# One wait per pair of rows for the diagonals' places on ScalarE, and a Gelu semaphore that counts rows

## The chip, the cores and the metric

The kernel runs on one core of a Trainium2 chip. The metric is the device time of one execution in microseconds (us). Before the change it is 900.75 us, the median of three runs (900.59 to 900.79 us).

## The reference

One decoder block over 256 positions of width 1024, all in float32. Its first half mixes tokens: a modulated RMS norm, one wide input projection, eight heads of forgetting attention and eight heads of causal ALiBi attention, sigmoid gates, an output projection and a gated residual. The change touches only the second half, PEER:

```
h2 = rms_norm(x, norm2_g) * (1 + scale2) + shift2
# per token and head: 16 of 16384 experts by two top-16 searches over 128 keys each
a = einsum('cd,chkd->chk', hc, u_tab[ec])      # dot with each chosen expert's u row
w = gc * gelu(a)                               # gc: softmax of the 16 scores of the head
y = einsum('chk,chkd->cd', w, v_tab[ec])       # weighted sum of the v rows
x = x + gate2 * y
```

With 8 heads and 16 experts a head each token reads 128 rows of u and 128 rows of v, 1024 floats each. The tables lie side by side in HBM, so that one row of 2048 floats holds u and v of an expert.

## The kernel before, in words

The tokens are two tiles of 128, one token to a partition. The engines are programmed one by one, each in its own written order, and meet at semaphores. After the attention and the projections comes the gather stage. It has 256 rows (`ROWS`): row n is expert number n % 128 of each token of tile n // 128, and it is 128 x 2048 floats, 1 MB.

- GpSimd (L594) gathers row n with an indirect DMA into one of 16 places of SBUF. A place is free again once TensorE has added the row that lay there (`s_added`), and the row's expert numbers must be there (`s_eid`).
- VectorE (`dots`, L1016) multiplies the landed u half with `h2` and sums it: `s_dot`.
- ScalarE (`weights_of`) makes from the dot the weight of the expert and a diagonal matrix of it: Gelu of the dots of two rows in one instruction (L1294, `s_gelu`), a product with the softmax value for each row (L1299, `s_ew`), and for each row a copy of the identity scaled by the weight into one of `ND` = 8 places of `diag` (L1306, `s_diag`). A place of `diag` is free once TensorE has added the row of eight rows before.
- TensorE (`add_rows`, L1620) multiplies the diagonal with the v half, two halves of 512 columns, and sums all 128 rows of a tile in PSUM. The profile shows four matmuls for a row, two for each half. It then tells `s_added`.
- After the last row of a tile VectorE (`finish`, L1027 and L1029) adds the gated sum to the residual and SP stores it.

ScalarE takes the rows in pairs (`expert_weights`), apart from the last 8 rows (`ALONE` = 4 pairs), which it takes one by one. Between the pairs of the stage other work is laid at fixed slots (`SLOT`): key queries and their scores on TensorE and ScalarE, the top-16 searches on VectorE up to slot 76, softmax parts on ScalarE. The expert numbers of later heads come out of that work while the rows of earlier heads are gathered.

In `weights_of` two waits stand ahead of each diagonal from row 8 on. ScalarE's instruction can carry one of them itself, and the other is an instruction of its own, which the profile shows as EVENT_SEMAPHORE at L1305. The first four pairs (rows 0 to 7) have no wait for a place.

Of the kernel before, what the change touches and what calls it, by code (L numbers as in the profile page):

```python
# [11 lines left out]
ACT = mybir.ActivationFunctionType  # L12
# [7 lines left out]
TOPK = 16  # L20
# [7 lines left out]
ND = 8  # L28
# [144 lines left out]
def block_kernel(nc, x, small, b_ada, b_fgate, norm2_g, ada_t, in_t, up_t, out_t, peer_t, keys_t, peer_uv, out):  # L173
# [21 lines left out]
    with ExitStack() as ctx:  # L195
        def sb(name, shape, dt=F32):
            return ctx.enter_context(nc.sbuf_tensor(name, shape, dt))

        def sem(name):
            return ctx.enter_context(nc.semaphore(name))  # L200
# [19 lines left out]
        diag = sb("diag", [P, ND, P])  # L220
# [54 lines left out]
        ident = sb("ident", [P, P])  # L275
# [16 lines left out]
        g_sb = sb("g_sb", [P, NG * TOPK])  # L292
# [3 lines left out]
        adot = mask[:, 0:2 * TOPK]  # L296
        gel = mask[:, 2 * TOPK:3 * TOPK]
        ew = mask[:, 3 * TOPK:4 * TOPK]
# [113 lines left out]
        s_dot = sem("dot_ready")  # L412
        s_added = sem("v_row_added")
        s_gelu = sem("gelu_ready")
        s_ew = sem("expert_weights_ready")
# [645 lines left out]
        def _(act):  # L1061
# [221 lines left out]
                gt = g_sb[:, t * P + h * TOPK:t * P + (h + nh) * TOPK]  # L1283
                act.activation(gt, gt, ACT.Exp).then_inc(s_g1, 1)

            gelus = [0]

            def weights_of(rows_):

                first, count = rows_[0], len(rows_)  # L1290
                at = first % (2 * TOPK)
                some = slice(first % TOPK, first % TOPK + count)
                act.wait_ge(s_dot, first + count)
                act.activation(gel[:, some], adot[:, at:at + count], ACT.Gelu_apprx_tanh).then_inc(s_gelu, 1)  # L1294
                gelus[0] += 1
                act.wait_ge(s_gelu, gelus[0])
                for n in rows_:
                    c_ = n % TOPK
                    act.activation(ew[:, c_:c_ + 1], g_sb[:, n:n + 1], ACT.Copy,  # L1299
                                   scale=gel[:, c_:c_ + 1]).then_inc(s_ew, 1)  # L1300
                for n in rows_:
                    c_ = n % TOPK
                    act.wait_ge(s_ew, n + 1)
                    if n >= ND:
                        act.wait_ge(s_added, n - ND + 1)  # L1305
                    act.activation(diag[:, n % ND, :], ident[:], ACT.Copy,  # L1306
                                   scale=ew[:, c_:c_ + 1]).then_inc(s_diag, 1)

            def expert_weights(pair):

                if pair >= NG * PAIRS - ALONE:
                    for n in (2 * pair, 2 * pair + 1):
                        weights_of((n,))
                else:
                    weights_of((2 * pair, 2 * pair + 1))

            behind = {}
            for t in range(TILES):
# [33 lines left out]
            for pair in range(NG * PAIRS):  # L1352
                expert_weights(pair)
                run(pair)
# [351 lines left out]
```

## Time and profile before

| what | us |
|---|---|
| median of three runs | 900.75 |
| profiled execution | 900.84 |
| its span | 899.0 |
| TensorE matmul busy | 779.8 |
| VectorE busy | 613.0 |
| ScalarE busy | 346.6 |
| GpSimd busy | 291.1 |

The span is the time from the first to the last instruction of the program. Matmuls overlap and their ends are modelled, so that TensorE's busy time is not its work at full speed. Waits, branches and DMA issues do not count as busy. The transfers are spread over 16 DMA engines; a DMA share of 1.00 says that all of them had packets under way all the time.

### The profile page before, as it was taken

To read this page: it belongs to the slowest core of one execution; us is meant where nothing else is said; L and a number is where in the kernel's file an instruction comes from. 1 tells how busy PE (TensorE), PEld (TensorE's weight loads), DVE (VectorE), ACT (ScalarE), POOL (GpSimd) and SP (SyncE) were. 2 spreads that over 40 slices of the span, in tenths; PEclk is the share of its full clock that TensorE was granted. 3 is DMA by queue.
4 is the path that set the end of the run, shared out by engine and by line. 5 is a ranking of instruction groups with operands and counts; after the bars stand their busy time and mean duration, and the time that the engine had idled before them with its cause. 6 is when DMAs were issued, how large, how long until landed. Compare 5 with 4: busy or idle time off the path is not lost.

```text
span 899.0 us, 8440 instructions
## 1 busy us (share of the span) xinstructions
PE 779.8 (87%) x2526; PEld 420.1 (47%) x2526; DVE 613.0 (68%) x1420; ACT 346.6 (39%) x1027; POOL 291.1 (32%) x279
## 2 busy tenths in 40 slices
PE   4999999999999999999997888787777777777777
PEld 2377877667556556565652333333323232223232
DVE  6788798964587967748669788668744444444445
ACT  3458687862244342423423232322322222222222
POOL 4000000000244454553546344453443434333320
PEclk9999999999999999999998888898899999999999
DMA  9978454689499999999999999999999999999995
GB/s 371 425 268 296 160 208 195 236 337 397 150 387 422 390 423 420 411 421 421 421 421 421 421 422 420 422 422 420 422 421 422 421 423 420 421 423 422 421 422 217
DMA packets 44100, 336.70 MB, mean 375 GB/s; under 512 B 4884, under 2 KB 5012, under 8 KB 7320
## 3 DMA queue, kind: packets, MB, share of 16 engines
q0 software_dynamic: 37152, 268.45, 72.1%
q1 hardware_dynamic: 6888, 67.72, 19.1%
q8 instruction: 20, 0.33, 0.1%
q14 instruction: 24, 0.20, 0.1%
q10 hardware_dynamic: 16, 0.00, 0.0%
HBM read 335.11 MB, written 1.05 MB: 374 GB/s over the span
## 4 chain that ended last, share of the span: by engine, by line
PE 49%; DMA 35%; DVE 10%; ACT 3%; issue 2%; POOL 1%; SPq 0%; DVEq 0%; POOLq 0%; ACTq 0%
DMA ring<-in_peer_uv,eid 26%; PE ps_y L1620 22%; DMA rows<-in_peer_uv,eid 6%; PE bank L1590 6%; PE bank L1556 3%; DVE ring L1016 3%; PE bank L1431 2%; PE bank L1433 2%; PE bank L1432 2%; DMA ring<-in_ada_t 2%; PE bank L1571 2%; PE ps_y L1431 1%; PE ps_y L1433 1%; PE ps_y L1432 1%; PE bank L1476 1%
## 5 line engine op out<-in xcount | busy, mean ns | idle before, releaser
L1620 PE MATMUL ps_y<-ring,diag 128*128 128x512 f32 x572 | 282.0, 634 | 57.2 <-ACT diag L1306 57.2
L594 POOL DMA_INDIRECT ring<-in_peer_uv,eid x142 | 159.0, 1119 | 421.5 <-DVE eid L922 225.0
L1016 DVE CUSTOM_DVE_ANT_0 ring<-ring,gates 128x1024 f32<-128x1024 f32 x143 | 173.3, 1225 | 102.3 <-DMA ring<-in_peer_uv,eid 101.5
L1620 PEld LDWEIGHTS ps_y<-ring,diag 128*128 128x128 f32 x572 | 111.5, 201 | 208.7 <-issue 122.2
L1294 ACT ACTIVATE mask<-mask 128x2 f32<-128x2 f32 (+1 forms) x132 | 26.7, 203 | 374.3 <-DVE mask L1016 374.1
L1306 ACT ACTIVATE diag<-ident,mask 128x128 f32<-128x128 f32 x256 | 87.3, 387 | 0.3
L1620 PE MATMUL ps_y<-rows,diag 128*128 128x512 f32 x136 | 61.8, 597 | 7.6 <-ACT diag L1306 7.6
L1299 ACT ACTIVATE mask<-g_sb,mask 128x1 f32<-128x1 f32 x256 | 61.9, 287 | 4.3
L1016 DVE CUSTOM_DVE_ANT_0 rows<-rows,gates 128x1024 f32<-128x1024 f32 x34 | 41.3, 1224 | 31.7 <-DMA rows<-in_peer_uv,eid 31.6
L651 DVE TENSOR_TENSOR w_lo<-ring,w_hi 128x512 fp32r<-128x512 f32 x76 | 50.8, 686 | 11.0 <-PE bank L1433 9.4
L1111 ACT ACTIVATE w_hi<-ring 128x512 fp32r<-128x512 f32 x76 | 45.6, 626 | 24.5 <-PE bank L1433 23.9
L636 DVE SCALAR_TENSOR_TENSOR rows<-ring,silu,rows 128x512 f32<-128x512 f32 x64 | 47.7, 749 | 3.3 <-DMA ring<-in_ada_t 2.2
L1620 PE MATMUL ps_y<-kz,diag 128*128 128x512 f32 x88 | 40.1, 598 | 5.6 <-ACT diag L1306 5.6
L1620 PEld LDWEIGHTS ps_y<-rows,diag 128*128 128x128 f32 x136 | 25.2, 190 | 41.9 <-issue 27.0
L594 POOL DMA_INDIRECT rows<-in_peer_uv,eid x34 | 35.5, 1043 | 26.7 <-PE ps_y L1620 21.1
L1620 PE MATMUL ps_y<-gates,diag 128*128 128x512 f32 x72 | 34.6, 602 | 7.7 <-ACT diag L1306 7.7
L1016 DVE CUSTOM_DVE_ANT_0 kz<-kz,gates 128x1024 f32<-128x1024 f32 x22 | 26.7, 1224 | 18.8 <-DMA kz<-in_peer_uv,eid 18.8
L1431 PE MATMUL bank<-w_hi,hT_hi 128*128 128x512 f32 x88 | 36.1, 410 | 0.0
L1433 PE MATMUL bank<-w_lo,hT_hi 128*128 128x512 f32 x88 | 34.3, 390 | 0.0
L1432 PE MATMUL bank<-w_hi,hT_lo 128*128 128x512 f32 x88 | 34.3, 390 | 0.0
L594 POOL DMA_INDIRECT kz<-in_peer_uv,eid x22 | 22.7, 1032 | 32.7 <-PE ps_y L1620 19.2
L1620 PE MATMUL ps_y<-spare,diag 128*128 128x512 f32 x52 | 25.2, 606 | 8.9 <-ACT diag L1306 7.6
(229 smaller groups left out, 1191.2 us busy)
## 6 DMA issues: line engine op xcount, KB each, us to landing
ring<-in_ada_t SPq DMA_DIRECT2D x11, 2048.0 KB, 9.8
ring<-in_in_t SPq DMA_DIRECT2D x10, 2048.0 KB, 10.5
ring<-in_up_t SPq DMA_DIRECT2D x2, 2048.0 KB, 7.7
ring<-in_out_t SPq DMA_DIRECT2D x2, 2048.0 KB, 10.8
ring<-in_peer_uv,eid POOLq DMA_INDIRECT x142, 28.6
x_sb<-in_x SPq DMA_DIRECT2D x2, 1024.0 KB, 10.1
ring<-in_ada_t SPq DMA_DIRECT2D x2, 1024.0 KB, 21.4
kz<-in_peer_t SPq DMA_DIRECT2D x1, 2048.0 KB, 19.2
```

The source lines that it names most:

```text
L594: pool.indirect_dma_start(uv_row(n), None, peer_uv, bass.IndirectOffsetOnAxis(ap=eid[:, n:n + 1], axis=0)).then_inc(s_uv[name], 16)
L636: ins = dve.scalar_tensor_tensor(out=acc, in0=w, scalar=silu[:, k:k + 1], in1=acc, op0=ALU.mult, op1=ALU.add)
L651: dve.tensor_tensor(w_lo[:, j % NLO, :], w, w_hi[:, j % NHI, :].bitcast(F32), ALU.subtract).then_inc(s_w_lo, 1)
L1016: dve.tensor_tensor_reduce(u_row(n), u_row(n), h2[:, n // P, :], 1.0, 0.0, ALU.mult, ALU.add, adot[:, at:at + 1]).then_inc(s_dot, 1)
L1111: act.activation(w_hi[:, j % NHI, :], ring[:, no % NW, k, :], ACT.Copy).then_inc(s_w_hi, 1)
L1299: act.activation(ew[:, c_:c_ + 1], g_sb[:, n:n + 1], ACT.Copy, scale=gel[:, c_:c_ + 1]).then_inc(s_ew, 1)
L1306: act.activation(diag[:, n % ND, :], ident[:], ACT.Copy, scale=ew[:, c_:c_ + 1]).then_inc(s_diag, 1)
L1431: pe.matmul(spot, hT_hi[:, k, at], hi, start=(k == 0), stop=False)
L1432: pe.matmul(spot, hT_lo[:, k, at], hi, start=False, stop=False)
L1433: ins = pe.matmul(spot, hT_hi[:, k, at], lo, start=False, stop=(k == KD - 1))
L1590: ins = pe.matmul(b[:, j * P:(j + 1) * P], peer_block(m // 2, k)[:, at:at + P], tT[:, t, k, :], start=(k == 0), stop=(k == KD - 1))
L1620: ins = pe.matmul(ps_y[:, cut], diag[:, n % ND, :], v_row(n)[:, cut], start=first, stop=last)
```

## The change

`weights_of` takes numbers (first row, how many, and the row for the semaphore counts) in place of a list. For a pair, it waits for a place of `diag` once, for the second row of the pair, and that wait stands ahead of the second product (L1299) and no longer ahead of the two diagonals. Since rows are added in order, that count covers the first row's place too. For a single row the wait stands ahead of its product. `s_gelu` goes up by the number of rows of the Gelu, and not by one.

```diff
-            gelus = [0]
-            def weights_of(rows_):
-                first, count = rows_[0], len(rows_)
+            def weights_of(first, count, row):
                 at = first % (2 * TOPK)
                 some = slice(first % TOPK, first % TOPK + count)
-                act.wait_ge(s_dot, first + count)
-                act.activation(gel[:, some], adot[:, at:at + count], ACT.Gelu_apprx_tanh).then_inc(s_gelu, 1)
-                gelus[0] += 1
-                act.wait_ge(s_gelu, gelus[0])
-                for n in rows_:
-                    c_ = n % TOPK
-                    act.activation(ew[:, c_:c_ + 1], g_sb[:, n:n + 1], ACT.Copy,
+                act.wait_ge(s_dot, row + count)
+                act.activation(gel[:, some], adot[:, at:at + count], ACT.Gelu_apprx_tanh).then_inc(s_gelu, count)
+                act.wait_ge(s_gelu, row + count)
+                for r in range(count):
+                    c_ = first % TOPK + r
+                    if r == count - 1 and first >= ND:
+                        act.wait_ge(s_added, row + (count - ND))
+                    act.activation(ew[:, c_:c_ + 1], g_sb[:, row + r:row + r + 1], ACT.Copy,
                                    scale=gel[:, c_:c_ + 1]).then_inc(s_ew, 1)
-                for n in rows_:
-                    c_ = n % TOPK
-                    act.wait_ge(s_ew, n + 1)
-                    if n >= ND:
-                        act.wait_ge(s_added, n - ND + 1)
-                    act.activation(diag[:, n % ND, :], ident[:], ACT.Copy,
+                for r in range(count):
+                    c_ = first % TOPK + r
+                    act.wait_ge(s_ew, row + (r + 1))
+                    act.activation(diag[:, (first + r) % ND, :], ident[:], ACT.Copy,
                                    scale=ew[:, c_:c_ + 1]).then_inc(s_diag, 1)
...
                     for n in (2 * pair, 2 * pair + 1):
-                        weights_of((n,))
+                        weights_of(n, 1, n)
                 else:
-                    weights_of((2 * pair, 2 * pair + 1))
+                    weights_of(2 * pair, 2, 2 * pair)
```

## Rows read from the trace of the kernel before

**Rows 1.** The kernel in three stretches: busy us of each engine, clock, DMA share, GB/s.
```profile
core 0: us, PE busy (x) PEld busy (x) DVE busy (x) ACT busy (x) POOL busy (x), PEclk, DMA share, GB/s
250.00:400.00 150.00, 147.45 (x621) 88.15 (x620) 113.66 (x308) 57.01 (x181) 78.39 (x64) 1.00 1.00 410
400.00:884.00 484.00, 391.97 (x950) 170.15 (x948) 306.20 (x717) 141.10 (x510) 197.55 (x189) 0.94 1.01 421
884.00:899.00 15.00, 9.39 (x20) 3.55 (x20) 7.60 (x12) 3.80 (x13) 0.00 (x0) 1.00 0.30 118
```

**Rows 2.** The last loop of the chain of waits: start us, us, what.
```profile
813.72 33.45 DMA ring<-in_peer_uv,eid
847.19 1.23 DVE ring L1016
849.51 2.00 PE ps_y L1620 x4
851.77 0.94 POOL extra L594
853.49 33.44 DMA ring<-in_peer_uv,eid
886.95 1.23 DVE ring L1016
889.23 4.57 PE ps_y L1620 x10
893.83 0.70 DVE tmp L1027
```

**Rows 3.** GpSimd in order of time, 489 to 499 us: start, us, idle before, releaser.
```profile
490.63 0.96 POOL L594 DMA_INDIRECT ring<-in_peer_uv,eid  x1 [0.60 <-PE ps_y L1620]
498.86 0.93 POOL L594 DMA_INDIRECT ring<-in_peer_uv,eid  x1 [7.27 <-PE ps_y L1620]
```

**Rows 4.** The stretch between these two gathers.
```profile
490.63:498.86 8.23, 4.05 (x5) 1.85 (x6) 6.50 (x14) 2.53 (x10) 0.96 (x1) 0.63 1.01 422
```

**Rows 5.** The waiting instruction of L1305 over the run: duration min/median/max, first and last start.
```profile
L1305 ACTq EVENT_SEMAPHORE  x248: 17/17/17, 280.9 to 890.9; - x124
```

**Rows 6.** ScalarE's first pair in order of time, rows 0 and 1, without L1305.
```profile
252.93 0.20 ACT L1294 ACTIVATE mask<-mask 128x2 f32<-128x2 f32 x1 [4.78 <-DVE mask L1016]
253.17 0.30 ACT L1299 ACTIVATE mask<-g_sb,mask 128x1 f32<-128x1 f32 x1
253.37 0.28 ACT L1299 ACTIVATE mask<-g_sb,mask 128x1 f32<-128x1 f32 x1
253.56 0.39 ACT L1306 ACTIVATE diag<-ident,mask 128x128 f32<-128x128 f32 x1
253.85 0.39 ACT L1306 ACTIVATE diag<-ident,mask 128x128 f32<-128x128 f32 x1
```

**Rows 7.** A later pair of ScalarE in order of time, with L1305 ahead of both diagonals.
```profile
602.98 0.20 ACT L1294 ACTIVATE mask<-mask 128x2 f32<-128x2 f32 x1 [3.67 <-DVE mask L1016]
603.22 0.29 ACT L1299 ACTIVATE mask<-g_sb,mask 128x1 f32<-128x1 f32 x1
603.42 0.28 ACT L1299 ACTIVATE mask<-g_sb,mask 128x1 f32<-128x1 f32 x1
603.61 0.39 ACT L1306 ACTIVATE diag<-ident,mask 128x128 f32<-128x128 f32 x1
603.90 0.39 ACT L1306 ACTIVATE diag<-ident,mask 128x128 f32<-128x128 f32 x1
```

**Rows 8.** ScalarE in order of time, one of the last eight rows.
```profile
885.72 0.20 ACT L1294 ACTIVATE mask<-mask 128x1 f32<-128x1 f32 x1 [1.52 <-DVE mask L1016]
885.96 0.29 ACT L1299 ACTIVATE mask<-g_sb,mask 128x1 f32<-128x1 f32 x1
886.29 0.40 ACT L1306 ACTIVATE diag<-ident,mask 128x128 f32<-128x128 f32 x1
```

**Rows 9.** From the start to 335.60 us: TensorE's matmuls of L1620, then ScalarE's L1299.
```profile
0.00:335.60 335.60, 51.86 (x117) 0.99 0.78 310
0.00:335.60 335.60, 7.89 (x34) 0.99 0.78 310
```

**Rows 10.** Who waited for ScalarE's diagonals, 250 to 400 us: total us, times, longest.
```profile
PEld ps_y L1620 <- ACT diag L1306: 6.0, 11, 2.2
PE ps_y L1620 <- ACT diag L1306: 1.9, 2, 1.4
```

**Rows 11.** VectorE: L983 for one head, then for two, each with its successor.
```profile
277.50 0.17 DVE L983 SCALAR_TENSOR_TENSOR eid<-score 128x16 int32<-128x16 f32 x1
277.59 0.16 DVE L986 TENSOR_REDUCE gsum<-g_sb 128x1 f32<-128x16 f32 x1
314.14 0.19 DVE L983 SCALAR_TENSOR_TENSOR eid<-score 128x32 int32<-128x32 f32 x1
314.25 0.18 DVE L986 TENSOR_REDUCE gsum<-g_sb 128x2 f32<-128x32 f32 x1
```

## The prediction, made before the changed kernel ran

> **What bounds the kernel now.** I read the stretches first, the chain of waits second, and then ScalarE instruction by instruction. From 400 to 884 us the DMA engines have packets all the time (share 1.01) and move 421 GB/s, while TensorE is busy 392 of 484 us, VectorE 306 and ScalarE 141 [rows 1]. A gathered row is 128 x 8192 bytes = 1.049 MB, so it takes 1.049 / 421 = 2.49 us, and 484 / 2.49 = 194 rows pass in that stretch. The transfers bound it. From 250 to 400 us the rate is 410 GB/s: (421 - 410) / 421 x 150 = 3.9 us worth of bytes fewer, and there TensorE is busy 147.5 of 150 us [rows 1]. What lies before 250 us has no instruction of the change. Behind 884 us come the last rows and the store.
>
> The chain of waits looks otherwise at first sight: it runs in loops from a transfer (33.4 us) over VectorE, ScalarE and TensorE to GpSimd, which issues the next transfer into the place that came free [rows 2]. One would think that a faster ScalarE shortens each loop. It does not: of the 33.4 us the row's own bytes need 2.49, and the rest is the queue of the rows issued before it. The plainest proof is a hole. After the gather at 490.63 GpSimd issues none until 498.86 us, since it sat 7.27 us waiting for TensorE to free a place [rows 3], and in just those 8.2 us the DMA engines moved 422 GB/s at a share of 1.01 [rows 4]. Where the DMA queue is full, a delay of several us between dot and gather costs nothing, and so an advance of some tens of ns gains nothing.
>
> **The change part by part.**
>
> *The waits that go.* There are 248 waiting instructions of L1305, one for each row from 8 on, of 17 ns each [rows 5]. From the rows that are left in pairs, 8 to 247, both waits of a pair go, 240 in all; the second product then has a wait of its own and nothing else ahead of it that would need an instruction beside it. The 8 single rows keep theirs. Together they are 240 x 0.017 = 4.1 us of ScalarE's sequencer. What are they worth to the engine? The kernel before has its own control: rows 0 to 7 have no such wait. In the first pair the instructions start at 253.17, 253.37, 253.56 and 253.85: steps of 0.20, 0.19 and 0.29 us [rows 6]. In a later pair, with both waits, they start at 603.22, 603.42, 603.61 and 603.90: the same 0.20, 0.19 and 0.29 us [rows 7]. The waits are worked off by the sequencer while the engine is still in the products ahead; ScalarE's own pace sets the steps. The gain is 0 in every pair; its bound, if a wait did show, is 2 x 0.017 = 0.034 us a pair.
>
> *The wait that is moved.* It now stands ahead of the second product. Queued behind it are that product and both diagonals of the pair, and for the diagonals TensorE waits. Two costs are possible. The first is that it holds. It asks for the row seven before the second of the pair to be added, so it holds only if TensorE is more than 8 rows behind ScalarE at that moment. The widest distance that I found is at 335.60 us: 34 products begun and 117 matmuls begun, at four a row 29 rows done [rows 9]. That is 5 rows against 8. The place waits never held, and the move makes the question come only 0.48 us earlier (603.42 against 603.90 for the second diagonal [rows 7]), where a row of TensorE takes four matmuls, 1.8 to 2.0 us (4.57 for ten, 2.00 for four [rows 2]). Cost 0. That cover is gone if TensorE falls three more rows behind. The first row's diagonal now also waits for one row more of TensorE than it did; with 5 outstanding rows this is as idle as the other.
>
> The second possible cost is of the wait that doesn't hold. The two products overlap: the second starts 0.09 us before the first ends (603.42 against 603.51), while an instruction that waits for the one ahead of it starts 0.03 to 0.04 us behind its end (603.22 after Gelu's end at 603.18 [rows 7]; 886.29 after 886.25 [rows 8]). If a wait on the second product broke the overlap, it would start at 603.55 and the pair's diagonals 0.13 us late. The nearest row is the second diagonal: it also has waits attached that are fulfilled before its turn, and it starts 0.10 us before the first one ends (603.90 against 604.00 [rows 7]). So I take 0, and keep 0.13 us a pair as the upper bound.
>
> *Gelu's count.* In a pair its semaphore goes up by 2. No instruction of ScalarE did this before. VectorE has it at L983: with one head the count goes up by one and the next instruction starts 0.09 us behind the start of L983, with two heads by two and 0.11 us behind, with twice the elements [rows 11]. I take 0. As an upper bound I let the second step of the count cost one more hop of 0.04 us, the gap between Gelu and the first product [rows 7]. In the single rows it goes up by 1 as before. The Trainium skill, in "Trainium Kernel Development and Optimization", section Key Constraints, says that compute semaphores must increment by 1; taken at its word it speaks against this edit, and gives no time but a kernel whose count falls short. This trace does not agree with that reading: the expert numbers' semaphore is raised by two for every pair of heads, and the gathers that count on it run to the end [rows 11].
>
> *The single rows at the end.* Behind the last landing the chain is dot, Gelu, product, diagonal, matmuls [rows 2, 8]. The wait for the place still is one instruction beside one that carries the other wait, now ahead of the product instead of the diagonal. Product behind Gelu and diagonal behind product both start 0.03 to 0.04 us after the end ahead of them, the second although it has the additional wait and the first although it has not [rows 8]. So moving it costs 0, and the tail, 899.0 - 886.95 = 12.1 us, stays.
>
> *Where a change per pair could show at all.* Not where the DMA queue is full. In the 150 us from 250 on, TensorE has 2.5 us of idle time in all [rows 1] and waited for a diagonal 2 times, its weight load 11 times [rows 10]. So at most 11 pairs could pass a change on. Gain: 11 x 0.034 = 0.4 us. Loss: 11 x (0.13 + 0.04) = 1.9 us.
>
> **The sum.** 0 for the waits that go, 0 for the moved one, 0 for the count, 0 at the end. The profiled execution took 900.84 us, 1.84 us around its span of 899.0, and it lies 0.09 us above the median of the runs. I predict the median, 900.7 us.
>
> **Rivals.** A difference counts from 0.2% on, which is 1.8 us: below 898.95 faster, above 902.55 slower.
>
> 1. *The sequencer paces ScalarE after all.* If all 240 waiting instructions lay on the path, 4.1 us would go: 896.7 us. For it speaks only that the chain goes through ScalarE in each loop; against it the equal steps with and without the waits, and the full DMA queue. If only the pairs that TensorE waited for profit, it is 900.84 - 0.4 = 900.4, which would not be told from no change. Chance of the first 0.02, of the second 0.05.
>
> 2. *The attached wait breaks the overlap of the two products, and the count by two adds a hop.* Each pair's diagonals then come 0.17 us late. It decides only where TensorE stands waiting for a diagonal and the DMA queue is not full, which is the 11 cases between 250 and 400 us: 900.84 + 1.9 = 902.7 us. For it: no row shows this instruction with a wait of another engine. Against it: the second diagonal's row, and that most of these 11 waits were of the weight load, which has slack (2 of the matmul itself). Chance 0.03.
>
> 3. *The moved wait holds.* TensorE must be 8 rows behind. Then the first diagonal comes up to one row of TensorE late, 1.8 to 2.0 us, but TensorE has seven rows before it and does not miss it. It gives 900.7 us and another look of the trace, since ScalarE would show idle time before L1299. Chance 0.02.
>
> 4. *The change does not do what it says.* If the waiting instructions stay because the two waits of another instruction are split up again, the count stays near 248 and the time at 900.7. Chance 0.03.
>
> The forecast itself has 0.85. Sums: same 0.85 + 0.05 + 0.02 + 0.03 = 0.95; faster 0.02; slower 0.03.
>
> **The range.** The forecast's own spread is the 0.2 us of the runs and the bound of 0.4 us of gain: 900.2 to 901.0. Toward loss I take in about half of the upper bound of 1.9 us, and as much for a small shift of the transfers in the stretch with the 3.9 us, either way: 900.0 to 901.8. The ends that are left out (896.7 and 902.7) have 0.05 together.
>
> **What would show it.** In the trace of the changed kernel: waiting instructions beside the products and diagonals number 8 and no longer 248; in a pair the three steps are again 0.20, 0.19 and 0.29 us (0.33 for the first of them would be the broken overlap); Gelu's end to the first product 0.04 us (0.08 is the hop); the stretch from 400 to 884 us again at 421 GB/s; ScalarE's L1299 without idle time ended by TensorE; the last loop of the chain has its dot near 886.95 and the span ends near 899.0. I am wrong if the stretch from 250 to 400 us moves noticeably less or more than 410 GB/s, or if the transfer rate itself differs.

## The result and the profile after

The changed kernel takes 902.02 us (median of 11 runs, 901.2 to 903.75), the kernel before 900.20 us in runs beside them (899.3 to 900.91). The ratio is 1.0022, 95% interval 1.0014 to 1.0030: slower by 2.0 us by the ratio, 1.8 us between the two medians. I had forecast no change, 900.7 us, range 900.0 to 901.8.

The profiled execution took 902.16 us with a span of 900.3. The stretches of the changed kernel follow, to be read against [rows 1]. Their columns are the stretch, its length, the busy time of TensorE, its weight loads, VectorE, ScalarE and GpSimd (all in us), TensorE's clock, the DMA share and GB/s.

```profile
250.00:400.00 150.00, 146.05 (x602) 86.33 (x601) 112.63 (x304) 57.87 (x182) 73.25 (x62) 0.99 0.99 404
400.00:884.00 484.00, 387.48 (x964) 169.60 (x963) 305.64 (x716) 139.60 (x507) 203.94 (x191) 0.96 1.01 421
```

From 400 us on the transfer rate does not differ: 421 GB/s in both. From 250 to 400 us it is 404 in place of 410 GB/s, which is 6 / 421 x 150 = 2.1 us worth of bytes. So the loss lies in the start of the gather stage. ScalarE's groups show why. Before ScalarE computes Gelu after another function, it loads Gelu's table, an instruction of its own (ACT_TABLE_LOAD). First the group of these loads ahead of Gelu in the kernel before, then the same group after (count, busy us in all, ns of one, idle us ahead of them and what ended it), then the waiting instructions after (count, duration in ns, first and last start):

```profile
L1294 ACT ACT_TABLE_LOAD x10 | 12.8, 1283 | 0.2
```

```profile
L1291 ACT ACT_TABLE_LOAD x10 | 12.8, 1283 | 31.7 <-DVE mask L1016 31.6
```

```profile
L1290 ACTq EVENT_SEMAPHORE  x124: 17/17/17, 252.0 to 874.6; - x124
L1296 ACTq EVENT_SEMAPHORE  x8: 17/17/17, 877.1 to 892.0; - x8
```

The 248 waits for places became 8 (L1296), as predicted. But 124 new ones came, at L1290: that is `wait_ge(s_dot, ...)`. Before, the Gelu instruction carried the wait for its dots itself. Now the update of a pair's Gelu adds 2 to the semaphore, and the wait is an instruction of its own. The two go together in the counts: 124 pairs add 2 and there are 124 such waits, while the 8 single rows add 1 and have none. The load of Gelu's table carries Gelu's line number, though the kernel does not ask for it, and stands right ahead of Gelu; it now stands behind that wait. Before, the load ran while ScalarE waited (0.2 us idle ahead of all ten loads); now ScalarE waits for VectorE's dots first (31.6 us ahead of them) and only then loads for 1.28 us.

Pair 4 (rows 8 and 9) is where it hurts. ScalarE in order of time, before and after:

```profile
277.37 1.28 ACT L1294 ACT_TABLE_LOAD   x1
280.61 0.20 ACT L1294 ACTIVATE mask<-mask 128x2 f32<-128x2 f32 x1 [1.96 <-DVE mask L1016]
281.23 0.68 ACT L1306 ACTIVATE diag<-ident,mask 128x128 f32<-128x128 f32 x2
```

```profile
279.68 1.28 ACT L1291 ACT_TABLE_LOAD   x1 [3.24 <-DVE mask L1016]
280.97 0.20 ACT L1291 ACTIVATE mask<-mask 128x2 f32<-128x2 f32 x1
281.60 0.68 ACT L1302 ACTIVATE diag<-ident,mask 128x128 f32<-128x128 f32 x2
```

The clocks of the two traces are shifted: the first gather starts at 236.23 before and at 235.26 after. Counted from it, the diagonals start at 45.00 before and 46.34 after, 1.34 us later: the load (1.28) and 0.06 of slower start. TensorE and GpSimd in the same stretch, before and then after:

```profile
281.67 3.70 PE L1620 MATMUL ps_y<-ring,diag 128*128 128x512 f32 x8 [1.41 <-ACT diag L1306]
286.36 0.94 POOL L594 DMA_INDIRECT ring<-in_peer_uv,eid  x1 [0.30 <-issue]
292.12 0.93 POOL L594 DMA_INDIRECT ring<-in_peer_uv,eid  x1 [4.82 <-PE ps_y L1620]
```

```profile
282.03 5.40 PE L1616 MATMUL ps_y<-ring,diag 128*128 128x512 f32 x8 [2.75 <-ACT diag L1302]
287.70 0.94 POOL L594 DMA_INDIRECT ring<-in_peer_uv,eid  x1 [1.94 <-PE ps_y L1616]
294.18 0.94 POOL L594 DMA_INDIRECT ring<-in_peer_uv,eid  x1 [5.54 <-PE ps_y L1616]
```

TensorE sat idle 2.75 us in place of 1.41, which is the 1.34. In this execution the clock also fell behind the gap: the eight matmuls took 5.40 in place of 3.70 us, and the granted clock of 280 to 300 us, below, is 0.91 in place of 1.00; from 284 to 286 us it is 0.50 (1.2 GHz instead of 2.4). The 22nd gather stands 55.89 us behind the first one before (292.12) and 58.92 us after (294.18): 3.03 us later, 1.34 from the gap and 1.7 from the clock. The queue of transfers could not cover that. Stretch 280 to 300 us, before, then after:

```profile
280.00:300.00 20.00, 18.56 (x94) 12.37 (x94) 14.19 (x49) 5.95 (x22) 9.82 (x9) 1.00 1.01 410
```

```profile
280.00:300.00 20.00, 17.94 (x74) 10.91 (x75) 11.16 (x43) 5.53 (x18) 8.90 (x8) 0.91 0.91 358
```

Bytes that are not moved there are not made up for later: the rate from 400 us on is 421 GB/s with and without the delay.

### The profile page after: what moved, and what is told of

It reads as the page before. It is cut to its first block, busy times and chain, and to the rows that moved or that the text cites. A ratio compares the mean times of both kernels' runs of the same rounds, so it can differ in the third digit from the quotient of the medians.

```text
span 900.3 us, 8324 instructions
## 1 busy us (share of the span) xinstructions
PE 775.0 (86%) x2526; PEld 418.2 (46%) x2526; DVE 612.9 (68%) x1420; ACT 345.4 (38%) x1027; POOL 293.1 (33%) x279
## 4 chain that ended last, share of the span: by engine, by line
PE 44%; DMA 35%; DVE 12%; ACT 4%; issue 2%; POOL 1%; another core or an unknown queue 0%; SPq 0%; ACTq 0%; DVEq 0%; POOLq 0%
DMA ring<-in_peer_uv,eid 29%; PE ps_y L1616 18%; DMA rows<-in_peer_uv,eid 6%; PE bank L1586 4%; DVE ring L1016 4%; PE bank L1552 3%; PE bank L1427 2%; PE bank L1428 2%; PE bank L1429 2%; PE bank L1567 2%; PE ps_y L1427 1%; PE ps_y L1391 1%; PE ps_y L1429 1%; PE ps_y L1428 1%; PE bank L1534 1%
## 5 line engine op out<-in xcount | busy, mean ns | idle before, releaser
L1616 PE MATMUL ps_y<-ring,diag 128*128 128x512 f32 x572 | 278.1, 626 | 58.6 <-ACT diag L1302 58.6
L1297 ACT ACTIVATE mask<-g_sb,mask 128x1 f32<-128x1 f32 x256 | 61.9, 287 | 4.4
L594 POOL DMA_INDIRECT rows<-in_peer_uv,eid x34 | 38.0, 1117 | 27.9 <-PE ps_y L1616 22.6
L1264 ACT ACTIVATE qp<-bank 128x256 f32<-128x256 f32 x16 | 6.1, 383 | 76.9 <-PE bank L1586 69.4
L1616 PE MATMUL ps_y<-extra,diag 128*128 128x512 f32 x48 | 23.6, 614 | 11.2 <-ACT diag L1302 11.2
```

What stands on the lines that cost most here:

```text
L594: pool.indirect_dma_start(uv_row(n), None, peer_uv, bass.IndirectOffsetOnAxis(ap=eid[:, n:n + 1], axis=0)).then_inc(s_uv[name], 16)
L1297: act.activation(ew[:, c_:c_ + 1], g_sb[:, row + r:row + r + 1], ACT.Copy, scale=gel[:, c_:c_ + 1]).then_inc(s_ew, 1)
L1616: ins = pe.matmul(ps_y[:, cut], diag[:, n % ND, :], v_row(n)[:, cut], start=first, stop=last)
```

## Experiments

All ratios are to runs of the kernel before on the same chip, with 95% intervals. An interval is some 0.8 us wide to either side, so a ratio of 1.0000 excludes the loss but not a few tenths of a us. In the code cuts `...` and the missing rest of a statement stand for code that is left out.

### One edit at a time

**Count by one, the moved wait kept.**

```diff
-                .then_inc(s_gelu, count)
-                act.wait_ge(s_gelu, row + count)
+                .then_inc(s_gelu, 1)
+                gelus[0] += 1
+                act.wait_ge(s_gelu, gelus[0])
```

`gelus = [0]` stands ahead of `weights_of` again, as in the kernel before.

> The changed kernel with its one moved wait for the places, but Gelu's semaphore goes up by one again. My theory (the count by two takes the wait for the dots off the Gelu instruction, and ten table loads then stand behind that wait): Gelu waits for the dots itself, all ten table loads run ahead of the dots, and the time is that of before, ratio 1.000 within 0.001. Rival A (the moved wait costs): the time stays that of the changed kernel, ratio 1.002. Rival B (the removed waits are worth something): ratio 0.999 or less.

Measured: 899.85 us, ratio 0.9999 (0.9990 to 1.0008). The ten loads stand ahead of the wait again, and the 240 waits are gone:

```profile
L1293 ACT ACT_TABLE_LOAD x10 | 12.8, 1283 | 0.2
```

So the moved wait and the removed ones together change nothing beyond the interval of 0.9 us; rivals A and B fall.

**Count by two alone**, in the kernel before: `.then_inc(s_gelu, count)` and `gelus[0] += count`.

> The kernel before, with both waits for the places where they were, and only Gelu's semaphore counting rows. My theory: it has all of the loss, ratio 1.002 (some 902 us), with the ten table loads behind the wait. Rival A (the moved wait costs): ratio 1.000.

Measured: 902.23 us, ratio 1.0024 (1.0015 to 1.0033), all of the loss:

```profile
L1294 ACT ACT_TABLE_LOAD x10 | 12.8, 1283 | 32.9 <-DVE mask L1016 32.9
```

### The load or the wait

**Count by two at the ten loads, and everywhere else.** In the kernel before, with `LOADS = (0, 2, 4, 11, 23, 35, 47, 55, 63, 75)`:

```diff
+                step = 2 if first // 2 in LOADS else 1
-                ....then_inc(s_gelu, 1)
-                gelus[0] += 1
+                ....then_inc(s_gelu, step)
+                gelus[0] += step
```

and in the other kernel `step = 2 if count == 2 and first // 2 not in LOADS else 1`.

> The kernel before with Gelu's semaphore going up by two only in the ten pairs ahead of whose Gelu a table load stands. My theory: these ten carry all of the loss, ratio 1.002. Rival C (every separate wait for the dots costs some tens of ns in its pair, 124 times): 10 of 124 pairs carry next to nothing, ratio 1.000.

> The kernel before with Gelu's semaphore going up by two in the other 114 pairs, where no table load stands. My theory: the separate wait without a load behind it costs under 0.1 us a pair, hidden in the transfers, ratio 1.000. Rival C: 114 of 124 pairs carry nearly all of the loss, ratio 1.002.

Measured: at the ten loads 902.80 us, ratio 1.0026 (1.0014 to 1.0039); everywhere else 900.07 us, ratio 0.9999 (0.9990 to 1.0008). The separate waits for the dots were there as meant, in the first 10, in the second 114:

```profile
L1296 ACTq EVENT_SEMAPHORE  x10: 17/17/17, 253.1 to 638.7; - x10
```

```profile
L1296 ACTq EVENT_SEMAPHORE  x114: 17/17/17, 256.4 to 872.6; - x114
```

The 114 separate waits cost nothing that shows, ten with a load behind them cost 2.3 us by the ratio (6 runs). Rival C falls.

**The table ahead of the wait**, in the changed kernel as it is:

```diff
+                if count == 2 and first // 2 in LOADS:
+                    act.activation(root_of_one[:], ones[:, 0:1], ACT.Gelu_apprx_tanh).then_inc(s_warm, 1)
                 act.wait_ge(s_dot, row + count)
```

> The changed kernel as it is, count by two and all, with a small Gelu of one column ahead of the wait for the dots in the ten pairs, so that the table is loaded before the wait again. My theory (it is the place of the ten table loads and nothing else): ratio to the kernel before 1.000. Rival D (the separate wait itself, or the addition to the count, costs where the transfers aren't full): ratio stays 1.002.

Measured: 900.08 us, ratio 1.0000 (0.9991 to 1.0009). ScalarE and TensorE at pair 4:

```profile
277.59 1.28 ACT L1293 ACT_TABLE_LOAD   x1
278.88 0.20 ACT L1293 ACTIVATE root_of_one<-ones 128x1 f32<-128x1 f32 x1
280.84 0.20 ACT L1295 ACTIVATE mask<-mask 128x2 f32<-128x2 f32 x1 [1.75 <-DVE mask L1018]
```

```profile
281.90 3.70 PE L1620 MATMUL ps_y<-ring,diag 128*128 128x512 f32 x8 [1.48 <-ACT diag L1306]
```

The gap of TensorE is 1.48 us, against 1.41 before and 2.75 in the changed kernel. Everything of the change is still in, the count by two too; only the place of the loads is back. Rival D falls.

### Which load

The kernel with `LOADS`, with other lists.

> The kernel before with the count by two in pair 4 alone, the load that stands near 278 us. The gather of row 20 came 1.3 us later against row 17's than before in the kernels with all ten. If this one load carries the loss: ratio 1.0015 to 1.0025. If the loss is spread over the ten: ratio 1.0002.

> The kernel before with the count by two in pairs 23, 35, 47, 55, 63 and 75 alone, the loads behind 370 us. My theory (with the queue of transfers full a late load is hidden, though four of them delay the pair by 1.3 us): ratio 1.000. Rival F (all loads count alike): six tenths of the loss, ratio 1.0014.

> The kernel before with the count by two in pair 11 alone, the load near 317 us, which in the kernel before starts behind ScalarE's copies and ends 1.02 us behind the dot. If every load in the stretch where the transfers aren't full counts: some 0.3 us, as its delay grows only from 1.02 to 1.36 us, ratio 1.0004. If only pair 4 counts: 1.0000.

> The kernel before with the count by two in pairs 0 and 2 alone, the loads near 252 and 266 us. Pair 0 comes 1.34 us late, pair 2 0.5 us late. My theory (a late pair counts where TensorE then has nothing else to do; at 252 us it works on the output product): ratio 1.000. Rival F (each late load in the early stretch is passed on to the end): ratio 1.002.

| pairs counted by two | us | ratio | 95% |
|---|---|---|---|
| 4 | 902.29 | 1.0025 | 1.0015 to 1.0034 |
| 23, 35, 47, 55, 63, 75 | 900.10 | 0.9999 | 0.9990 to 1.0008 |
| 11 | 900.75 | 1.0010 | 1.0001 to 1.0019 |
| 0, 2 | 899.72 | 1.0000 | 0.9991 to 1.0009 |

Pair 4 alone has the whole loss. TensorE and GpSimd with it:

```profile
282.18 3.70 PE L1623 MATMUL ps_y<-ring,diag 128*128 128x512 f32 x8 [2.76 <-ACT diag L1309]
292.63 0.94 POOL L596 DMA_INDIRECT ring<-in_peer_uv,eid  x1 [5.54 <-PE ps_y L1623]
```

```profile
280.00:300.00 20.00, 17.79 (x88) 11.86 (x89) 12.86 (x45) 6.56 (x22) 9.32 (x8) 1.00 0.97 382
```

The gap is 2.76 us again. This execution kept its clock (3.70 us for eight matmuls), and the 22nd gather comes 57.22 us behind the first one (at 235.41), 1.33 later than before.

The late loads are hidden, as the full queue says. All six stood behind the wait, four of them (near 496, 533, 574 and 636 us) made their pair 1.3 us late, and nothing followed. One of them, near 533 us:

```profile
533.14 1.28 ACT L1297 ACT_TABLE_LOAD   x1 [5.43 <-DVE mask L1018]
534.44 0.20 ACT L1297 ACTIVATE mask<-mask 128x2 f32<-128x2 f32 x1
```

At pair 0 the delay is as large, but TensorE is in the output product then and does not stand waiting. Its first matmuls of L1623 start 20.86 us behind the first gather (256.69 against 235.83), exactly as in the kernel before (257.09 against 236.23):

```profile
248.53 7.46 PE L1574 MATMUL bank<-ring,tT 128*128 128x512 f32 x17
```

Pair 11 measured 1.0010 where I expected 1.0000 or 1.0004. Its interval holds 1.0004 and just misses 1.0000, so a small part of the loss at this pair is neither shown nor excluded.

### The other way round

**Table even earlier.** The kernel before with a Gelu of one column behind the root and behind each softmax exponential, `act.activation(root_of_one[:], ones[:, 0:1], ACT.Gelu_apprx_tanh)`.

> The kernel before, and the small Gelu right behind the root and behind each softmax exponential, so that the table comes back before ScalarE waits for the key queries of the same slot. In the kernel before the Gelus of pairs 2, 11 and 23 start 0.85, 1.02 and 1.68 us behind their dots since the load stands behind those copies. My theory (delays at the start of the stage, where the queue of transfers is not yet full, are passed on): 0.5 to 1 us faster, ratio 0.999. Rival E (only delays of over 1 us at one place matter): ratio 1.000.

Measured: 900.29 us, ratio 1.0002 (0.9993 to 1.0011). My expectation of 0.999 was wrong: pairs 2, 11 and 23 had been late without harm, and pair 4, whose load was already covered in the kernel before, gained nothing.

**Pair 4 one by one, and pairs 0 to 11 one by one.**

```diff
-                if pair >= NG * PAIRS - ALONE:
+                if pair >= NG * PAIRS - ALONE or pair == 4:
```

and `or pair < 12` in the second.

> The kernel before with the two rows of pair 4 taken one by one, as the last eight are. TensorE then gets row 8's diagonal some 1.0 us earlier (its dot is there 1.14 us ahead of row 9's), where it sat idle 1.41 us. My theory (pair 4 is the place whose delay goes to the end): 0.7 to 1.1 us faster, ratio 0.999. Rival G (the place hurts when late but has no gain, since another wait is as late): ratio 1.000.

> The kernel before with the rows of pairs 0 to 11 one by one. More Gelus, and each row's diagonal as soon as its dot is there. If pair 4 is the only place: as with pair 4 alone, 0.999. If the other pairs of the start pass on their part too: 0.998 or less. If the additional Gelus delay ScalarE's copies for TensorE: 1.000 or more.

Measured: pair 4 alone 899.21 us, ratio 0.9991 (0.9982 to 1.0000); twelve pairs 899.46 us, ratio 0.9998 (0.9989 to 1.0007). TensorE, GpSimd and the stretch with pair 4 one by one:

```profile
280.22 3.70 PE L1620 MATMUL ps_y<-ring,diag 128*128 128x512 f32 x8 [0.23 <-ACT diag L1306]
290.67 0.93 POOL L594 DMA_INDIRECT ring<-in_peer_uv,eid  x1 [3.64 <-PE ps_y L1620]
```

```profile
280.00:300.00 20.00, 19.75 (x99) 13.34 (x100) 15.31 (x53) 6.56 (x25) 9.59 (x8) 1.00 1.01 421
```

TensorE's gap fell from 1.41 to 0.23 us, and the 22nd gather stands at 54.70 us behind the first (at 235.97) in place of 55.89. The median is 0.7 us below the 899.87 of before in the same runs, but the interval of the ratio reaches 1.0000, and the twelve pairs, whose 22nd gather stands at 54.71 us, measured 0.9998. So the earlier gather is shown, and a gain in time is not.

All fourteen traces put pair 4 on one scale. The last column is the time from the first gather to the end of the span:

| traces | TensorE's gap | 22nd gather | GB/s, 280 to 300 | GB/s, 250 to 400 | to the end |
|---|---|---|---|---|---|
| pair 4 one by one (2) | 0.23 | 54.70, 54.71 | 421, 419 | 415, 416 | 662.5, 661.6 |
| load ahead of the wait (8) | 1.41 to 1.48 | 55.89 to 55.96 | 403 to 419 | 410 to 413 | 662.0 to 663.0 |
| load behind the wait, clock kept (3) | 2.75, 2.76 | 57.22, 57.23 | 382 to 391 | 407, 408 | 663.7 to 664.2 |
| changed kernel, clock fell | 2.75 | 58.92 | 358 | 404 | 665.0 |

At one and the same gap the rate from 280 to 300 us varies from 403 to 419, so that the 421 with pair 4 one by one says little by itself.

## Why the prediction was wrong

**What failed** is the step *Gelu's count*: "I take 0. As an upper bound I let the second step of the count cost one more hop of 0.04 us". The question was put wrongly. I asked what the update costs after the instruction, and read from VectorE's L983 [rows 11]: nothing. I did not ask what the update does to the wait ahead of the instruction. The count by two took the wait off Gelu and put it in front of the table load, and the price was 1.34 us at a load (1.28 of load, 0.06 of slower start), paid in time at pair 4 alone as far as the runs can tell. The rows for it were in the trace of before: ten table loads of 1283 ns with 0.2 us idle ahead of them, which says that each ran under the wait for the dots. I never listed that row among the things hidden by a wait that the change touches. The prediction even says that what lies before 250 us has no instruction of the change, while the first of these loads (L1294) starts at 246.88.

The control that I used held the answer too. In the kernel before, L983 runs nine times, twice with a count of one and seven times with a count of two. The wait ahead of it (L611, in a helper that waits for the step before) is an instruction of its own exactly seven times, the first right ahead of the L983 at 314.14 [rows 11]:

```profile
L611 DVEq EVENT_SEMAPHORE  x7: 21/21/21, 314.1 to 633.7; - x7
```

The reduction ahead of L983, for one head and then for two, shows the delay too:

```profile
276.78 0.69 DVE L980 TENSOR_REDUCE score<-tmp 128x32 f32<-128x512 f32 x1
312.82 1.22 DVE L980 TENSOR_REDUCE score<-tmp 128x64 f32<-128x1024 f32 x1
```

L983 starts 0.03 us behind the end of the first (277.47 to 277.50) and 0.10 us behind the end of the second (314.04 to 314.14). So the trace of before already showed that a count by two goes with a separate wait and a start some 0.07 us later, ahead of the instruction and not behind it.

The hop that I bounded at 0.04 us did not come where I put it, behind Gelu: Gelu ends at 604.62 and the first product starts at 604.65, 0.03 us. One came ahead of Gelu: in the changed kernel a dot ends at 604.33 and its Gelu starts at 604.42, 0.09 us, where it was 602.95 and 602.98, 0.03. The experiment with 114 such waits shows that these 0.06 us a pair are hidden. The row of VectorE above had about this size.

```profile
604.25 0.08 DVE L1016 DVE_READ_ACCUMULATOR2_ANT mask<- 128x1 f32 x1
604.42 0.20 ACT L1291 ACTIVATE mask<-mask 128x2 f32<-128x2 f32 x1 [3.68 <-DVE mask L1016]
```

**What held.** The waits that go: 240 are gone and worth 0 (0.9999 with the moved wait alone). The moved wait: 0 as well (the row that it asks for is eight before the second of the pair, not seven as the prediction has it, which changes nothing in the sum). The steps of a pair after the change are 604.65, 604.86 and 605.04, 0.21 and 0.18 us in place of 0.20 and 0.19 [rows 7], and the products still overlap, 604.86 against 604.94. Rival 3 did not come up: ScalarE never waited for TensorE ahead of L1297. The full queue hides all behind 400 us: right, and shown directly by the late loads. The tail: right, 12.03 us from the dot that starts at 888.27 to the end of the span, as against 12.05.

```profile
604.65 0.29 ACT L1297 ACTIVATE mask<-g_sb,mask 128x1 f32<-128x1 f32 x1
604.86 0.28 ACT L1297 ACTIVATE mask<-g_sb,mask 128x1 f32<-128x1 f32 x1
605.04 0.39 ACT L1302 ACTIVATE diag<-ident,mask 128x128 f32<-128x128 f32 x1
```

**Where a change could show.** I had bounded this to the pairs that TensorE waited for between 250 and 400 us [rows 10] and priced the loss at 11 x 0.17 = 1.9 us. The place was right: of the 2 waits of the matmul itself the larger, 1.41 us, is pair 4. The size was not an addition of eleven small delays but one delay of 1.34 us. Rival 2 named 902.7 us, near the measured 902.0, but with another mechanism (a broken overlap, which did not occur), so it gets no credit for the number. Rival 4 asked whether the waiting instructions would stay; it looked at the right kind of row and at the wrong wait.

The Trainium skill, in "Trainium Kernel Development and Optimization", section Key Constraints, asks for increments of 1 for compute semaphores. I had read it as a rule about a count that falls short and dismissed it. The runs show no short count, but a ratio of 1.0024 for the count by two alone, so to keep to it would have avoided the loss here; it names neither the moved wait nor the table load. In "ScalarE: Activation LUTs", section What ACT_TABLE_LOAD costs, it gives some 1283 ns for the load itself, as the traces do.

**What stays open.** The delay at pair 4 is 1.34 us and the measured loss 2.0 to 2.3 us by the ratios. Of the four traces with pair 4 late, one (the changed kernel) had a stretch at 1.2 GHz behind the gap, which put 1.7 us on top; the three others (count by two alone, at the ten loads, at pair 4 alone) kept their clock. Counted from the first gather to the end, these three take 1.2 to 1.8 us more than the 662.5 us that is the mean of the eight traces with the load ahead of the wait, and the changed kernel 2.6 us. If a quarter of the executions had the stretch, the loss would be some 1.8 us on average, an estimate from these traces that lies within the intervals. How many of the timed runs had it is not known, and nothing was tried to hold the clock up. The rest, some 0.2 us above the 1.34, is not explained.

## What to carry to other kernels

An edit of a semaphore can change which instruction carries a wait, and what the compiler inserts ahead of an instruction then changes sides. Before an edit near a wait, list what runs under that wait at no cost now, table loads first. And look for the stall at the stage's start, where the queue of transfers is not yet full and where the engine that frees the places (here TensorE) already stands waiting. A microsecond at such a place reached the end, while the same delay at pair 0, where TensorE had other work, and a hundred separate waits without a load behind them cost nothing that shows. A count by two that the kernel already has, as at L983 here, shows in the trace of before what it does to a wait.

## What the runs showed of the hardware

An instruction of ScalarE or VectorE whose update added 2 had its wait as an instruction of its own: on ScalarE 124, 114, 10, 6, 2 and 1 times in the changed kernel and the experiments, on VectorE 7 times in the kernel before, each time as many as there were such updates. Where the engine really waits, the instruction then starts 0.09 us behind the one that it waits for (ScalarE) and 0.10 us (VectorE), in place of 0.03. In the kernels here that alone cost no time that shows (0.9999 with 114 of them).

A wait of TensorE of 2.75 us was followed by some 3.4 us at half clock in one execution (1.7 us more for eight matmuls) and not in three others (2.75, 2.76 and 2.76 us). The same happened near 32 us, long before the change. In both traces TensorE waits 0.68 and 1.00 us there; then the 16 matmuls of the next product take 8.80 us in the kernel before and 7.10 in the changed one. The clock from 20 to 40 us, below for the changed kernel and then for the one before, is 1.00 and 0.91. The first gather comes 0.97 us earlier in the changed kernel (235.26 against 236.23). Over all fourteen traces the seven with 0.91 have their first gather at 235.97 to 236.39, the seven with 1.00 at 235.00 to 235.83, 0.8 us earlier on average. That is a part of the spread between executions of one kernel, and why times in two traces are compared from the first gather on.

```profile
20.00:40.00 20.00, 18.32 (x47) 5.95 (x46) 14.32 (x28) 8.66 (x19) 0.00 (x0) 1.00 1.02 432
```

```profile
20.00:40.00 20.00, 18.26 (x43) 5.58 (x41) 14.80 (x29) 8.80 (x19) 0.00 (x0) 0.91 1.02 430
```
